# Grid attention of a four-block transformer kernel: values stationary in column halves, probabilities normalised first, attention gates projected turned

## The chip, the cores and the metric

One core of one Trainium2 chip runs the whole program in one launch. The time is the device time of one execution in microseconds (us); lower is better. Three runs of the kernel before took 1077.77, 1074.63 and 1081.78 us, median 1077.77.

## The reference

The reference applies a first block of two layers (retention, sparse attention and a gated linear attention, merged by gates) to 256 tokens of width 1024, and then a second block of two layers to these 256 tokens and 256 context tokens. The change lies in the second block's first layer, `even_layer`. Cut to what matters, for 512 rows (four tiles of 128: tiles 0 and 1 are the sequence, 2 and 3 the context):

```python
q, k, v, u, vv, gate = split(h @ w_in)         # widths 512, 128, 128, 512, 512, 1024
# 8 heads of 64, 2 key/value heads; a learned sink logit for each head
s = [q @ k.T * scale (masked to a window for the sequence), sink]
p = softmax(s)[..., :-1]                       # the sink takes its share, and is dropped
a = p @ v                                      # 512 wide
b = gelu(u) * spatial_mix(layer_norm(gelu(vv)))# 512 wide
y = (concat([a, b]) * silu(gate)) @ w_out      # 1024 -> 1024
x = x + gate_ada * y
```

A sequence tile attends to all four tiles under a mask, a context tile to the two context tiles.

## The kernel before, in words

Five instruction streams are written out by hand: SyncE issues the weight transfers into a ring of three 2 MB slots, TensorE multiplies, VectorE and ScalarE evacuate the eight PSUM banks, GpSimd does a little. Every PSUM use is a named unit in a fixed list (`units_of_layer_e` for this layer): the list sets which bank a unit has and, bank by bank, the order. `filled(engine, unit)` waits until TensorE has written a unit, `emptied` until its reader has freed the bank. Each engine's stream is in the order in which it is written; nothing overtakes.

Projections that must be exact to float32 are made of three products of a faster type: `hi*hi`, `hi*rest`, `low*hi`. For that ScalarE copies each operand into a rounded high half (`wide_high`, L1709) and VectorE subtracts it from the original to get the low half (`wide_low`, L2508). A weight chunk comes in four pieces, and `project_wide` (L1113) waits for piece k/2 before its products 3k. Its stationary operand is the tokens' 128x128 block, its moving one 512 weight columns: 24 products a tile.

The grid attention runs in 15 steps, the loops over `E_STEPS` in the streams of TensorE (L1240), ScalarE (L1769) and VectorE (L2589). There are 24 units: one head of a sequence tile over 512 keys (0 to 15), or two heads of a context tile over 256 keys each (16 to 23). Step g handles:

- the gate projection of `E_GATES`: attention half (`e_g0`) in steps 0 to 3, the other half (`e_g1`) in steps 7 to 10, one tile a step; ScalarE takes its tanh, VectorE makes silu of it in `eg` (`e_silu`);
- modulation rows (`ada_rows`, `ada`, `mod_out`) in steps 5 to 11 and two row products (`gate_rows`) in each of steps 11 and 12, in banks 0 and 1 by turns with the gates;
- the transposes of units 2g-4 and 2g-3 (`e_turn`), copied out by ScalarE into `PT2e`;
- the logits of units 2g and 2g+1 (`e_logits_pair`), which VectorE evacuates with the mask (L2602) and reduces to the maximum (L2605), or reduces straight from PSUM (L2609); ScalarE then takes the exponential in place with the row sum (L1789, L1794);
- the values of units 2g-6 and 2g-5 (`e_values`): stationary is the transposed block of probabilities, 128x128, moving are 64 columns of `ev`;
- in step 4 the spatial gate's products (L1275), four units of two products in banks 0 and 1, multiplied out of PSUM by VectorE (L2631);
- the split of the next gate or output weights: ScalarE in steps 4, 5, 10, 11; VectorE in steps 5, 6 (`e_g1`), 11 and 12 (first output half).

The probabilities are not normalised before the values: `e_gated` (L2546) adds the sink's exponential to the row sums, takes the reciprocal, multiplies a tile's 512 attended columns out of PSUM by it, and then by the gate. The tile's 1024 mixed columns are turned with eight transposes in two banks (`turn_mixed`), split into high (`mixed_high`) and low (`mixed_low`) halves, and projected (`project_mixed`): tile 0 in step 14, the rest behind the loop. The float32 products of attention appear as two instructions each in the trace, the transposes as one. The second attention, in the layer after (`o_values` L1372, `o_normal` L2721), already has normalised probabilities moving over stationary values.

Of the kernel before, what the change touches and what calls it, by code (L numbers as in the profile page):

```python
# [215 lines left out]
def units_of_layer_e():  # L216
# [17 lines left out]
    for g in range(E_STEPS):  # L234
# [63 lines left out]
def build(nc, x, weights, cols, k1, gmask, ident_in, wlr, context, k2, out):  # L298
    ctx = ExitStack()
    with ctx:  # L300
# [142 lines left out]
        eg = sbe("eg", [P, NT, D])  # L443
# [25 lines left out]
        etmp = evv[:, 0, :]  # L469
# [69 lines left out]
        def e_rows(name):  # L539
            return eg[:, int(name[-1]), 0:512] if name in E_EARLY.values() else msum2[E_ROWS.index(name) % 2]  # L540
# [163 lines left out]
        def _(pe):  # L704
# [420 lines left out]

            def project2(u, name, slot, t, width):
# [59 lines left out]
            def e_turn(i):  # L1186
                if E_UNITS[i][0] < TT:
                    pe.wait_ge(event("e_exp"), i + 1)
                else:
                    emptied(pe, u, f"el{i}")  # L1190
                ps = begin(u, f"ep{i}")
                done(u, f"ep{i}", turn_blocks(ps, [L2e[:, i % 4, b * P:(b + 1) * P] for b in range(4)]))

            def e_values(i):
                emptied(pe, u, f"ep{i}")
                t, heads = E_UNITS[i]
                b0 = 0 if t < TT else TT
                nb = NT - b0
                if i == 0 or E_UNITS[i - 1][0] != t:
# [6 lines left out]
                if i == E_LAST[t]:  # L1206
# [18 lines left out]
            def turn_mixed(t):  # L1225

                pe.wait_ge(event("em_ready"), t + 1)
                pe.wait_ge(event("eb_ready"), t + 1)
                for h in range(2):
                    ps = begin(u, f"eyT{t}{h}")  # L1230
                    done(u, f"eyT{t}{h}", turn_blocks(ps, [eg[:, t, (4 * h + i) * P:(4 * h + i + 1) * P] for i in range(4)]))

            def project_mixed(h, t):

                if h == 0:
                    emptied(pe, u, f"eyT{t}0")
                    emptied(pe, u, f"eyT{t}1")
                project_wide(u, f"eout{t}{h}", 2 + h, t)

            for g in range(E_STEPS):  # L1240
                if g in E_GATES:
                    n, t = E_GATES[g] // 4, E_GATES[g] % 4
                    project_wide(u, f"e_g{n}{t}", n, t)
# [18 lines left out]
                if g >= 3:  # L1262
                    e_values(2 * g - 6)
                    e_values(2 * g - 5)
# [133 lines left out]
        def _(act):  # L1398
# [322 lines left out]
            def mixed_high(t):  # L1721

                for h in range(2):
                    ps = filled(act, u, f"eyT{t}{h}")
                    act.activation(xhi[:, 4 * h:4 * h + 4, t * P:(t + 1) * P], ps[:, :].rearrange("p (k c) -> p k c", k=4),
                                   ACT.Copy).then_inc(event("yhi_ready"), 1)
# [42 lines left out]
            for g in range(E_STEPS):  # L1769
                if g in E_GATES:  # L1770
                    n, t = E_GATES[g] // 4, E_GATES[g] % 4
                    ps = filled(act, u, f"e_g{n}{t}")
                    act.activation(eg[:, t, n * 512:(n + 1) * 512], ps[:, :], ACT.Tanh, scale=0.5).then_inc(event("e_tanh"), 1)
# [9 lines left out]
                if g < 12:  # L1783
                    for i in (2 * g, 2 * g + 1):
# [6 lines left out]
                        else:  # L1791
# [6 lines left out]
                            ins.then_inc(free(u, f"el{i}"), 1)  # L1798
                for j, n in {4: ((1, 0), (1, 1)), 5: ((1, 2), (1, 3)), 10: ((2, 0), (2, 1)), 11: ((2, 2), (2, 3))}.get(g, ()):
# [3 lines left out]
                for t in range(NT):  # L1803
                    if g == E_LAST[t] // 2 + 1:
                        act.wait_ge(event("e_arg"), t + 1)
                        act.activation(es2[:, t, :], es2[:, t, :], ACT.Exp).then_inc(event("e_es"), 1)
# [216 lines left out]
        def _(dve):  # L2023
# [521 lines left out]

            def e_gated(t):  # L2546

                dve.wait_ge(event("e_es"), t + 1)
                if t < TT:
# [340 lines left out]
```

## Time and profile before

| | |
|---|---|
| profiled execution | 1075.43 us |
| its span in the trace | 1073.5 us |
| granted TensorE clock, mean | 0.996 |
| TensorE busy | 1037.6 us, 97% |
| VectorE busy | 600.8 us, 56% |
| ScalarE busy | 477.8 us, 45% |
| GpSimd busy | 76.4 us, 7% |

The page gives each engine's busy time, the span in forty slices, the chain of waits that ended last, and the costliest groups of instructions by line and shape. PE is TensorE's matmul stream, PEld its weight loads (which overlap it), DVE is VectorE, ACT is ScalarE. A matmul's recorded length holds its latency, so instructions in a row overlap in the record: their price is the distance from one start to the next. The same holds, to 0.08 us, on VectorE.

### The profile page before, as it was taken

The page shows a single profiled execution, that of the slowest core. Times are in us where ns is not written, and L with a number is a line of the kernel's source. Part 1 is how long each engine was busy: PE and PEld are TensorE (multiplying, and loading weights), DVE is VectorE, ACT ScalarE, POOL GpSimd, SP SyncE. Part 2 cuts the span into 40 slices and gives each one's busy share as a digit, 9 for nine tenths or more (in the row PEclk, how much of TensorE's full clock was granted, in tenths as well). Part 3 has the DMA queues.
Part 4 walks back from the last instruction along what each step waited for, and adds up shares of the span by engine and source line. Part 5 has one row for each costly group of instructions (what it writes and reads, how often), then busy time and mean ns, then how long its engine had stood idle before and what let it go on. Part 6 is the DMA issues. An engine that isn't in the chain of part 4 may idle for free.

```text
span 1073.5 us, 13401 instructions
## 1 busy us (share of the span) xinstructions
PE 1037.6 (97%) x5148; PEld 751.6 (70%) x5148; DVE 600.8 (56%) x1177; ACT 477.8 (45%) x942; POOL 76.4 (7%) x103
## 2 busy tenths in 40 slices
PE   7999999999999999999999999999999999999997
PEld 5788875777466887757774587777677888556553
DVE  2539866595756299764455744235745555245742
ACT  3436546562144375375630353245535423225641
POOL 3001110000000021100000000500000001230000
PEclk9999999999999999999999999999999999999999
DMA  9844442477615454326467352431642016242000
GB/s 387 315 197 158 157 158 79 157 313 296 250 55 196 178 198 173 124 112 233 170 251 288 135 222 79 157 108 70 235 157 104 1 40 228 106 157 99 1 1 39
DMA packets 13742, 171.27 MB, mean 160 GB/s; under 512 B 1504, under 2 KB 1760, under 8 KB 3056
## 3 DMA queue, kind: packets, MB, share of 16 engines
q1 hardware_dynamic: 13216, 168.82, 41.2%
q10 hardware_dynamic: 464, 1.61, 0.4%
q8 instruction: 41, 0.67, 0.3%
q14 instruction: 21, 0.17, 0.0%
HBM read 169.37 MB, written 1.05 MB: 159 GB/s over the span
## 4 chain that ended last, share of the span: by engine, by line
PE 83%; DVE 7%; ACT 7%; DMA 2%; issue 1%; SPq 0%; DVEq 0%; ACTq 0%
PE bank L785 15%; PE bank L1123 8%; PE bank L1072 8%; PE bank L1012 7%; PE bank L1170 6%; PE bank L756 5%; PE bank L1129 5%; PE bank L1105 4%; PE bank L763 3%; PE bank L1307 3%; PE bank L857 3%; PE bank L1384 2%; PE bank L719 2%; PE bank L1372 1%; PE bank L727 1%
## 5 line engine op out<-in xcount | busy, mean ns | idle before, releaser
L1496 ACT ACTIVATE whi<-ring 128x512 fp32r<-128x512 f32 x120 | 73.8, 629 | 67.7 <-PE bank L785 67.5
L785 PE MATMUL bank<-whi,xhi 128*128 128x512 f32 (+1 forms) x256 | 99.2, 388 | 1.3 <-ACT dsag L1419 1.3
L2160 DVE TENSOR_TENSOR wlo<-ring,whi 128x512 fp32r<-128x512 f32 x120 | 82.2, 707 | 29.7 <-ACT whi L1496 29.4
L785 PE MATMUL bank<-whi,xlo 128*128 128x512 f32 (+1 forms) x256 | 97.9, 382 | 0.0
L785 PE MATMUL bank<-wlo,xhi 128*128 128x512 f32 (+1 forms) x256 | 97.4, 381 | 0.0
L763 PE MATMUL bank<-ring,hT 128*128 128x512 f32 (+1 forms) x160 | 61.8, 540 | 1.8 <-ACT hT L1439 1.8
L1129 PE MATMUL bank<-ring,hT 128*128 128x256 f32 (+2 forms) x224 | 57.9, 418 | 3.3 <-ACT hT L1462 2.3
L1012 PE MATMUL bank<-merge_high,xhi 128*128 128x512 f32 x144 | 58.5, 406 | 1.6 <-ACT retqkv L1419 1.1
L1012 PE MATMUL bank<-merge_high,xlo 128*128 128x512 f32 x144 | 57.0, 396 | 0.0
L785 PEld LDWEIGHTS bank<-whi,xhi 128*128 128x128 f32 x256 | 48.1, 188 | 12.7 <-ACT dsag L1419 1.6
L1012 PE MATMUL bank<-ring_low,xhi 128*128 128x512 f32 x144 | 56.7, 394 | 0.0
L785 PEld LDWEIGHTS bank<-wlo,xhi 128*128 128x128 f32 x256 | 48.2, 188 | 9.9
L785 PEld LDWEIGHTS bank<-whi,xlo 128*128 128x128 f32 x256 | 48.1, 188 | 9.9
L1129 PEld LDWEIGHTS bank<-ring,hT 128*128 128x128 f32 x224 | 38.9, 190 | 21.4 <-issue 16.3
L2349 DVE TENSOR_TENSOR ring_low<-ring,merge_high 128x1024 fp32r<-128x1024 f32 x36 | 42.5, 1222 | 18.8 <-ACT merge_high L1596 18.6
L1123 PE MATMUL bank<-ring_low,xhi 128*128 128x512 f32 x128 | 50.4, 394 | 0.0
L763 PEld LDWEIGHTS bank<-ring,hT 128*128 128x128 f32 x160 | 29.7, 190 | 28.6 <-issue 20.1
L1654 ACT ACTIVATE out_high<-ring 128x1024 fp32r<-128x1024 f32 x16 | 15.6, 1045 | 65.4 <-DMA ring<-in_weights 65.4
L2061 DVE SCALAR_TENSOR_TENSOR retqkv<-ring,cst,retqkv 128x512 f32<-128x512 f32 x56 | 42.1, 752 | 2.0
L1596 ACT ACTIVATE merge_high<-ring 128x1024 fp32r<-128x1024 f32 x36 | 36.0, 1052 | 9.7 <-PE bank L1012 9.7
L1123 PE MATMUL bank<-wide,xhi 128*128 128x512 f32 x96 | 39.0, 406 | 0.2 <-DVE ring_low L2511 0.2
L1170 PE MATMUL bank<-whi,xhi 128*128 128x512 f32 x96 | 38.4, 400 | 0.0
(412 smaller groups left out, 2182.4 us busy)
## 6 DMA issues: line engine op xcount, KB each, us to landing
ring<-in_weights SPq DMA_DIRECT2D x73, 2048.0 KB, 8.1
ring<-in_weights SPq DMA_DIRECT2D x5, 1024.0 KB, 5.1
ring<-in_weights SPq DMA_DIRECT2D x2, 1360.0 KB, 10.0
ring<-in_weights SPq DMA_DIRECT2D x1, 1536.0 KB, 8.7
kk<-in_k SPq DMA_DIRECT2D x1, 1120.0 KB, 8.1
X<-in_x SPq DMA_DIRECT2D x1, 1024.0 KB, 14.7
kc<-in_k ACTq DMA_DIRECT2D x1, 1024.0 KB, 11.9
X<-in_context SPq DMA_DIRECT2D x1, 1024.0 KB, 10.0
```

The lines of the kernel that those rows point to most:

```text
L756: mm = pe.transpose(ps[0:n, i * P:(i + 1) * P], blk, ident[:])
L763: mm = pe.matmul(ps[:, 0:width], hT[:, k, t * P:(t + 1) * P], ring[:, slot, k * width:(k + 1) * width], start=(k == 0), stop=(k == KD - 1))
L785: mm = pe.matmul(o[:, 0:width], a, b[:, q % BUFFERS, at], start=(k == 0 and m == 0), stop=(k == KD - 1 and m == 2))
L1012: mm = pe.matmul(o[:, :], a, b, start=(k == 0 and n == 0), stop=(k == KD - 1 and n == 2))
L1072: mm = pe.matmul(ps[:, :], branchT[b][:, k, t * P:(t + 1) * P], ring[:, slot, k * D + h * 512:k * D + h * 512 + 512], start=(k == 0), stop ...
L1105: mm = pe.matmul(ps[:, :], a, b, start=(k == 0 and m == 0), stop=(k == KD - 1 and m == 2))
L1123: mm = pe.matmul(ps[:, :], a, b, start=(k == 0 and n == 0), stop=(k == KD - 1 and n == 2))
L1129: mm = pe.matmul(ps[:, 0:width], hT2[:, k, t * P:(t + 1) * P], ring[:, slot, k * width:(k + 1) * width], start=(k == 0), stop=(k == KD - 1))
L1170: mm = pe.matmul(o[:, :], a, b, start=(k == 0 and m == 0), stop=(k == KD - 1 and m == 2))
L1496: act.activation(whi1[:, q % BUFFERS, :], w, ACT.Copy).then_inc(event("hi1_ready"), 1)
L2160: dve.tensor_tensor(wlo1[:, q % BUFFERS, :], piece1(q)[2], whi1[:, q % BUFFERS, :], ALU.subtract).then_inc(event("lo1_ready"), 1)
L2349: dve.tensor_tensor(rest, w, whole, ALU.subtract).then_inc(event("merge_low"), 1)
```

## The change

The values become the stationary operand, 128x64, in the left or right half of the array's columns by the parity of the head, and the transposed probabilities move over them, 128 columns at a time; two units (an even and an odd head) alternate product by product. The result is the attended block turned: head dimension on partitions, tokens in columns. For that the probabilities are normalised before they are turned (`e_normal`, VectorE, once a step for the step before), and the sink's argument and exponential are computed once a step for two or four heads (L2615 and L1806 before, once a tile). The gates' attention half is projected turned as well (`gates_e`: weights stationary, all 512 tokens moving). The gate is then multiplied in one instruction, and the high and low halves for the output projection are made from SBUF (`attended_high`, `attended_low`); only the other 512 columns are transposed, into one bank instead of two.

Where the pieces stand: `gates_e` in steps 0 to 3 on TensorE; the wait for `ea_low` in `project_mixed`, for h = 0; ScalarE's exponential of the sink behind each step's exponentials, `attended_high` in steps 9, 11, 14 and behind the loop; on VectorE `e_normal(g - 1)` at the head of steps 1 to 12, the sink's argument in every step behind the maxima, `e_gated` in steps 8, 10, 13 and behind the loop as before, `attended_low` in steps 10, 12, 14 and behind the loop.

```diff
     def units_of_layer_e():
         if g in E_TURNED:
-            u += [(f"eyT{E_TURNED[g]}{h}", (4, 0)[E_TURNED[g]] + h) for h in range(2)]
-    u += [(f"eyT{t}{h}", (4, 0)[t % 2] + h) for t in range(2, NT) for h in range(2)]
+            u.append((f"eyT{E_TURNED[g]}", (5, 1)[E_TURNED[g]]))
+    u += [(f"eyT{t}", (5, 1)[t % 2]) for t in range(2, NT)]
...
-        eg = sbe("eg", [P, NT, D])
+        egT = sbe("egT", [P, 4, NT * P])
+        eb = sbe("eb", [P, NT, 512])
...
+            def gates_e(j):
+                ps = begin(le, f"e_g0{j}")
+                for k in range(KD):
+                    if k % 2 == 0:
+                        pe.wait_ge(event("wide_low"), k // 2 + 1)
+                    at = k * 512 + j * P
+                    whole, rest = wide[:, k, j * P:(j + 1) * P], ring_low[:, SLOT2["e_g0"], at:at + P]
+                    for n, (a, b) in enumerate(((whole, xhi), (rest, xhi), (whole, xlo))):
+                        mm = pe.matmul(ps[:, :], a, b[:, k, :], start=(k == 0 and n == 0), stop=(k == KD - 1 and n == 2))
+                done(le, f"e_g0{j}", mm)
...
             def e_turn(i):
-                if E_UNITS[i][0] < TT:
-                    pe.wait_ge(event("e_exp"), i + 1)
-                else:
-                    emptied(pe, u, f"el{i}")
+                pe.wait_ge(event("e_norm"), i + 1)
...
-            def e_values(i):
+            def e_values(g):
+                units = (2 * g, 2 * g + 1)
...
-                for a, h in enumerate(heads):
+                for a in range(len(E_UNITS[units[0]][1])):
                     for b in range(nb):
-                        mm = pe.matmul(o[:, h * 64:(h + 1) * 64], PT2e[:, i % 4, (a * nb + b) * P:(a * nb + b + 1) * P],
-                                       ev[:, b0 + b, (h // 4) * 64:(h // 4) * 64 + 64], start=(b == 0), stop=(b == nb - 1))
+                        for r, i in enumerate(units):
+                            h = E_UNITS[i][1][a]
+                            mm = pe.matmul(o[64 * r:64 * r + 64, (h // 2) * P:(h // 2 + 1) * P],
+                                           ev[:, b0 + b, (h // 4) * 64:(h // 4) * 64 + 64],
+                                           PT2e[:, i % 4, (a * nb + b) * P:(a * nb + b + 1) * P],
+                                           start=(b == 0), stop=(b == nb - 1))
...
             def turn_mixed(t):
-                pe.wait_ge(event("em_ready"), t + 1)
                 pe.wait_ge(event("eb_ready"), t + 1)
-                for h in range(2):
-                    ps = begin(u, f"eyT{t}{h}")
-                    done(u, f"eyT{t}{h}", turn_blocks(ps, [eg[:, t, (4 * h + i) * P:(4 * h + i + 1) * P] for i in range(4)]))
+                ps = begin(u, f"eyT{t}")
+                done(u, f"eyT{t}", turn_blocks(ps, [eb[:, t, i * P:(i + 1) * P] for i in range(4)]))
...
+                    pe.wait_ge(event("ea_low"), t + 1)
...
+            def attended_high(t):
+                emptied(act, u, f"eo{t}")
+                c = slice(t * P, (t + 1) * P)
+                act.activation(xhi[:, 0:4, c], egT[:, :, c], ACT.Copy).then_inc(event("ea_high"), 1)
...
+                    act.wait_ge(event("e_arg"), g + 1)
+                    t, heads = step_heads(g)
+                    act.activation(es2[:, t, heads], es2[:, t, heads], ACT.Exp).then_inc(event("e_es"), 1)
...
+            def e_normal(g):
+                t, heads = step_heads(g)
+                dve.wait_ge(event("e_es"), g + 1)
+                if t < TT:
+                    dve.wait_ge(event("e_exp"), 2 * g + 2)
+                else:
+                    emptied(dve, u, f"el{2 * g}")
+                    emptied(dve, u, f"el{2 * g + 1}")
+                step(dve.tensor_tensor(r2[:, t, heads], sm2[:, t, heads], es2[:, t, heads], ALU.add))
+                settle()
+                step(dve.reciprocal(r2[:, t, heads], r2[:, t, heads]))
+                settle()
+                for i in (2 * g, 2 * g + 1):
+                    n = 512 // len(E_UNITS[i][1])
+                    for a, h in enumerate(E_UNITS[i][1]):
+                        v = L2e[:, i % 4, a * n:(a + 1) * n]
+                        ins = dve.tensor_scalar(v, v, r2[:, t, h:h + 1], None, ALU.mult)
...
             def e_gated(t):
-                step(dve.tensor_tensor(r2[:, t, 0:8], sm2[:, t, 0:8], es2[:, t, :], ALU.add))
-                step(dve.reciprocal(r2[:, t, 0:8], r2[:, t, 0:8]))
-                dve.tensor_tensor(etmp.rearrange("p (h d) -> p h d", h=8), ps[:, :].rearrange("p (h d) -> p h d", h=8),
-                                  r2[:, t, 0:8].unsqueeze(2).broadcast_to([P, 8, 64]), ALU.mult).then_inc(free(u, f"eo{t}"), 1)
-                dve.scalar_tensor_tensor(eg[:, t, 0:512], etmp, 0.5, eg[:, t, 0:512], ALU.mult, ALU.mult).then_inc(event("em_ready"), 1)
+                v = egT[:, :, t * P:(t + 1) * P]
+                dve.scalar_tensor_tensor(v, ps[:, :].rearrange("p (j c) -> p j c", j=4), 0.5, v, ALU.mult,
+                                         ALU.mult).then_inc(free(u, f"eo{t}"), 1)
+
+            def attended_low(t):
+                dve.wait_ge(event("ea_high"), t + 1)
+                c = slice(t * P, (t + 1) * P)
+                dve.tensor_tensor(xlo[:, 0:4, c], egT[:, :, c], xhi[:, 0:4, c], ALU.subtract).then_inc(event("ea_low"), 1)
...
-                for t in range(NT):
-                    if g == E_LAST[t] // 2:
-                        dve.wait_ge(event("e_max"), E_LAST[t] + 1)
-                        dve.tensor_tensor(es2[:, t, :], mx2[:, t, 0:8], sink, ALU.add).then_inc(event("e_arg"), 1)
+                    dve.wait_ge(event("e_max"), 2 * g + 2)
+                    t, heads = step_heads(g)
+                    dve.tensor_tensor(es2[:, t, heads], mx2[:, t, heads], sink[:, heads], ALU.add).then_inc(event("e_arg"), 1)
```

## Rows read from the trace of the kernel before

**Rows 1.** The page: busy us, share of the span, instructions of each engine.

```profile
PE 1037.6 (97%) x5148; PEld 751.6 (70%) x5148; DVE 600.8 (56%) x1177; ACT 477.8 (45%) x942; POOL 76.4 (7%) x103
```

**Rows 2.** Busy time by stretch (columns in its first line), steps 4 and 5.

```profile
core 0: us, PE busy (x) PEld busy (x) DVE busy (x) ACT busy (x) POOL busy (x), PEclk, DMA share, GB/s
755.00:771.00 16.00, 14.76 (x102) 10.44 (x100) 11.86 (x26) 8.18 (x17) 0.00 (x0) 1.00 0.56 222
```

**Rows 3.** The chain of waits, 754 to 784: start us, us, what.

```profile
754.23 0.70 DVE hT L2602
...
757.39 0.17 DVE es L2615
...
758.95 0.61 DVE hT L2602
...
761.99 0.80 DVE eu L2631 x2
...
769.05 0.70 DVE hT L2602
...
777.55 1.15 DVE ring_low L2511
```

**Rows 4.** Timeline of TensorE, 757 to 776: start us, us, what [idle before].

```profile
758.00 2.00 PE L1204 MATMUL bank<-ev,hT 128*128 128x64 f32 x16
759.84 1.95 PE L1275 MATMUL bank<-evv,ring 128*128 128x256 f32 x8
762.83 1.99 PE L1275 MATMUL bank<-evv,ring 128*128 128x256 f32 x8 [1.04 <-DVE eu L2631]
...
775.52 0.48 PE L1123 MATMUL bank<-wide,xhi 128*128 128x512 f32 x1
```

**Rows 5.** Weight loads of two lines (ns min/median/max), and timeline of tiled products.

```profile
L1204 PEld LDWEIGHTS bank<-ev,hT x192: 186/192/193, 754.1 to 845.1; 128*128 128x128 f32 x192
...
L1372 PEld LDWEIGHTS bank<-LP,ova x128: 132/137/137, 989.8 to 1036.6; 128*64 128x64 f32 x128
...
489.44 0.71 PE L940 MATMUL bank<-Y,KL 64*128 64x128 f32 x8
490.09 0.50 PE L1012 MATMUL bank<-merge_high,xhi 128*128 128x512 f32 x1
...
996.98 1.95 PE L1372 MATMUL bank<-LP,ova 128*64 128x256 f32 x16
998.86 1.09 PE L756 MATMUL bank<-ident,LP 128*128 128x128 f32 x8
```

**Rows 6.** Timeline of ScalarE: the end of step 3's exponentials.

```profile
758.02 0.19 ACT L1789 ACTIVATION_READ_ACCUMULATOR hT<-hT,mx 128x1 f32 x1
```

**Rows 7.** Timeline of VectorE: steps 3 and 11, and the second attention.

```profile
752.94 0.69 DVE L2570 SCALAR_TENSOR_TENSOR eg<-eg,bank 128x512 f32<-128x512 f32 x1 [1.87 <-ACT eg L1773]
...
829.27 4.62 DVE L2511 TENSOR_TENSOR ring_low<-ring,wide 128x1024 fp32r<-128x1024 f32 x4
...
983.22 0.89 DVE L2729 TENSOR_SCALAR LP<-LP,r 128x512 f32<-128x512 f32 x2
984.01 1.28 DVE L2736 TENSOR_REDUCE mx<-bank 128x1 f32<-128x512 f32 x2
```

**Rows 8.** The chain of waits, 815 to 845.

```profile
822.27 0.17 DVE r L2553
...
822.70 0.70 DVE evv L2558
...
824.15 0.18 DVE mod L2048
...
838.11 5.57 PE bank L1123 x24
```

**Rows 9.** Timeline of TensorE, steps 12 and 13.

```profile
831.85 1.90 PE L1204 MATMUL bank<-ev,hT 128*128 128x64 f32 x16
833.58 1.04 PE L756 MATMUL bank<-ident,eg 128*128 128x128 f32 x8
834.46 1.04 PE L756 MATMUL bank<-ident,hT 128*128 128x128 f32 x8
```

More of the change, by code:

```diff
@@ L539, in e_rows, with step_heads @@
         def e_rows(name):
-            return eg[:, int(name[-1]), 0:512] if name in E_EARLY.values() else msum2[E_ROWS.index(name) % 2]
+            return egT[:, int(name[-1]), :] if name in E_EARLY.values() else msum2[E_ROWS.index(name) % 2]
+        def step_heads(g):
+            t, heads = E_UNITS[2 * g]
+            return t, slice(heads[0], E_UNITS[2 * g + 1][1][-1] + 1)
         def e_which(name):
@@ L1242, in _ @@
                     n, t = E_GATES[g] // 4, E_GATES[g] % 4
-                    project_wide(u, f"e_g{n}{t}", n, t)
+                    if n == 0:
+                        gates_e(t)
+                    else:
+                        project_wide(u, f"e_g1{t}", 1, t)
                 if g in E_SUMS:
@@ L1262, in _ @@
                 if g >= 3:
-                    e_values(2 * g - 6)
-                    e_values(2 * g - 5)
+                    e_values(g - 3)
                 if g in E_TURNED:
@@ L1721, in mixed_high @@
             def mixed_high(t):
[L1723 to L1726, printed above, removed]
+                ps = filled(act, u, f"eyT{t}")
+                act.activation(xhi[:, 4:KD, t * P:(t + 1) * P], ps[:, :].rearrange("p (k c) -> p k c", k=4),
+                               ACT.Copy).then_inc(event("yhi_ready"), 1)
+            def attended_high(t):
+                emptied(act, u, f"eo{t}")
+                c = slice(t * P, (t + 1) * P)
+                act.activation(xhi[:, 0:4, c], egT[:, :, c], ACT.Copy).then_inc(event("ea_high"), 1)
             def e_sums_out(name):
@@ L1772, in _ @@
                     ps = filled(act, u, f"e_g{n}{t}")
-                    act.activation(eg[:, t, n * 512:(n + 1) * 512], ps[:, :], ACT.Tanh, scale=0.5).then_inc(event("e_tanh"), 1)
+                    act.activation((eb if n else egT)[:, t, :], ps[:, :], ACT.Tanh, scale=0.5).then_inc(event("e_tanh"), 1)
                 if g in E_SUMS:
@@ L2544, in spatial_norm @@
                 dve.tensor_tensor(evv[:, t, :], evv[:, t, :], lnb, ALU.add).then_inc(event("ln_ready"), 1)
[L2546 to L2563 removed]
+            def e_normal(g):
[3 more added lines that the diff above has]
+                    dve.wait_ge(event("e_exp"), 2 * g + 2)
+                else:
+                    emptied(dve, u, f"el{2 * g}")
[9 more added lines that the diff above has]
+                        ins = dve.tensor_scalar(v, v, r2[:, t, h:h + 1], None, ALU.mult)
+                        if a < len(E_UNITS[i][1]) - 1:
+                            step(ins)
+                    ins.then_inc(event("e_norm"), 1)
@@ L2568, in e_silu @@
                 ps = filled(dve, u, f"e_g{n}{t}")
-                v = eg[:, t, n * 512:(n + 1) * 512]
+                v = (eb if n else egT)[:, t, :]
                 dve.scalar_tensor_tensor(v, v, 1.0, ps[:, :], ALU.add, ALU.mult).then_inc(free(u, f"e_g{n}{t}"), 1)
@@ L2576, in e_mixed @@
                 emptied(dve, u, f"e_g1{t}")
-                v = eg[:, t, 512:1024]
+                v = eb[:, t, :]
                 dve.scalar_tensor_tensor(v, eu[:, t, :], 0.5, v, ALU.mult, ALU.mult).then_inc(event("eb_ready"), 1)
             def mixed_low(t):
-                for h in range(2):
-                    dve.wait_ge(event("yhi_ready"), 2 * t + h + 1)
-                    ps = filled(dve, u, f"eyT{t}{h}")
-                    c = slice(t * P, (t + 1) * P)
-                    dve.tensor_tensor(xlo[:, 4 * h:4 * h + 4, c], ps[:, :].rearrange("p (k c) -> p k c", k=4),
-                                      xhi[:, 4 * h:4 * h + 4, c], ALU.subtract).then_inc(free(u, f"eyT{t}{h}"), 1)
+                dve.wait_ge(event("yhi_ready"), t + 1)
+                ps = filled(dve, u, f"eyT{t}")
+                c = slice(t * P, (t + 1) * P)
+                dve.tensor_tensor(xlo[:, 4:KD, c], ps[:, :].rearrange("p (k c) -> p k c", k=4),
+                                  xhi[:, 4:KD, c], ALU.subtract).then_inc(free(u, f"eyT{t}"), 1)
             for g in range(E_STEPS):
+                if 1 <= g < 13:
+                    e_normal(g - 1)
                 if g in E_GATES:
@@ L2639, in _ @@
                     e_gated({8: 0, 10: 1, 13: 2}[g])
+                if g in (10, 12, 14):
+                    attended_low({10: 0, 12: 1, 14: 2}[g])
                 if g in E_TURNED:
@@ L2657, in _ @@
                             mixed_low(t + 2)
+                            if t == 0:
+                                attended_low(3)
                         elif t == 2:
```

30 lines of the change are left out of this document (11 added, 19 removed).

## The prediction, before the result was known

> **What bounds the kernel now.** I read the page's busy times first: TensorE is busy for 97% of the span [rows 1], so any work taken from it looks like time won. The change lies in the grid attention, about 725 to 888 us. The second view, busy time by stretch, already warns [rows 2]: at 755 to 771 TensorE is idle for 1.24 us of 16 while VectorE works 11.86, and the granted clock is 1.00, so no idle time is to be blamed on the clock. The third view settles it. The chain of waits [rows 3] runs through VectorE, not TensorE, from 754.23 to 762.78 (evacuations, maxima, two layer-norm instructions, the next step's evacuations, the first spatial-gate product), then through VectorE again from 769.05 to 778.70. Its last pieces there are the low half of a gate weight, for which TensorE's gate waits. TensorE is 97% busy and yet, in steps 4 to 6, VectorE sets its pace: from 754.23 to 763 it has next to no gap. The question is therefore what the change adds to VectorE ahead of those two points, and not only what it takes from TensorE.
>
> **What is removed from TensorE.** *Values.* There are 96 products, each two instructions, so 16 instructions in each of 12 steps. Now one step costs 1.84 us (758.00 to 759.84) [rows 4], in the last three steps 1.73 (831.85 to 833.58) [rows 9]. That is 0.115 us for 64 moving columns, while a full-width product with 256 columns costs 0.22 (eight in 1.99 with the last one's tail, from 762.83) [rows 4]. So it isn't the columns that cost here, but the 128-column weight load: 192 ns in length, against 137 for 64 columns [rows 5]. Afterwards the same 16 instructions have 64-column weights, 128 moving columns, and alternate between the two column halves of the array. The nearest row is the second attention's value product, with the same form and 256 columns: 16 in 1.88 us (996.98 to 998.86) [rows 5], 0.235 for a pair, about the price of one full-width instruction with 256 columns. The halves thus run side by side. With half the columns a pair costs about 0.11, and eight pairs 0.86; I take 1.0 us with the 0.12 to 0.16 us that the row has over eight times its streaming. From the other side, the row-halved product with 128 moving columns and 128-column loads took 0.65 us for eight (489.44 to 490.09) [rows 5], 1.3 us for 16; and no gain at all is 1.84. I take 1.0, since a 64-column load is the shorter one. Saved: 9 x 0.84 + 3 x 0.73 = 9.8 us.
>
> The pair row also speaks against a rule: 16 loads of the two halves lie beside streaming, as a pair costs no more than streaming its 256 columns. The Trainium skill (TensorE: Matmul & The Clock Gate, What overlaps and what doesn't) has a weight load overlap a running product only where its row group differs, and column halves share their row groups; the trace disagrees. By that rule load and streaming of a pair would add, about the 1.3 us a step of the row-halved product, and the change would give the third rival's time.
>
> *Transposes.* The mixed rows are now turned with 8 transposes a tile, 0.88 us (833.58 to 834.46) [rows 9]. Half of them go: 4 x 0.44 = 1.8 us.
>
> *Gates.* The attention half is projected turned: again 4 x 24 products, 128-column weights, 512 moving columns, and the same waits for weight pieces. Cost 0.
>
> TensorE loses 9.8 + 1.8 = 11.5 us of work (rounded once).
>
> **What is added to VectorE.** *Normalising*, once a step, at the head of the next step's queue: an addition and a reciprocal, 0.43 together (822.27 to 822.70) [rows 8], and the scaling of two 128x512 blocks in place. The second attention does just that scaling: two in 0.79 us (983.22 to 984.01) [rows 7]. So 1.22 us in steps 1 to 8. In the last four groups it is four blocks of 128x256, a form with no row: between half of 0.395 and all of it; I take 0.25 each, 1.4 us in all (bounds 1.2 and 2.0). *The sink's argument*, now in every step: 0.2 (0.17 at 757.39, and 0.02 of issue ahead of it) [rows 3], new in 8 of 12. *Gating* falls from four instructions, 1.88 us (822.27 to 824.15) [rows 8], to one of 0.65 (its 0.69 in the rows of that form less the overlap with the next). The low halves for the output projection stay 8 in number, four of them now from SBUF: no change. ScalarE gets 8 more small exponentials (under 0.2 each) and keeps its 8 high halves; it is busy for 8.18 of the 16 us of the tightest stretch [rows 2], so 0. SP and the weight transfers aren't touched; slots come free with TensorE's projections and move with them.
>
> New waits: VectorE now waits for ScalarE's exponentials before evacuating the next logits. In step 3 these end at 758.21 [rows 6], VectorE reaches the wait at 758.95 [rows 3]: no stall. In step 4 and after it gets there later still.
>
> **The walk**, each shift against the time before:
> - Steps 0 to 3: VectorE has a gap of 1.87 us ahead of its gate product [rows 7] and takes the 1.4 in. 0.
> - Step 4: it is back to back from 754.23. Group 3's scaling and one argument come ahead of the first spatial-gate evacuation: +1.42. TensorE, 1.68 us early from two cheaper value steps, waits longer instead: it goes on at 764.25, not 762.83, and into step 5 at +1.42.
> - Steps 5 and 6: TensorE would reach step 7's gate at 775.52 + 1.42 - 1.68 = 775.3 and want the third weight piece 12 products later, 2.8 us by the gate's 5.57 for 24 [rows 8], at 778.1. That piece was ready at 778.70. Ahead of it VectorE now has +1.42, two arguments and group 5's scaling: 0.4 + 1.22, in all +3.04, ready at 781.8. The gate ends 3.04 late. The four value steps have won nothing.
> - Steps 7 to 9: VectorE waits for gates here, so 3 x 0.84 is real: +0.52 at step 10's logits.
> - Step 11: the second row product waits for VectorE to empty a bank (824.15 and 0.18) [rows 8]. Before that now: -1.88 + 1.26 (gating and a low half) + 0.2 (argument) + 1.4 (group 10's scaling) = +0.98. Shift +1.50.
> - Step 13: the last group's turn needs its scaling, which stands behind step 11's three weight pieces. The pieces start at 829.27 and take 3.46 of the 4.62 for four [rows 7]: 832.73 + 1.50, and 0.43 + 0.5 for the first unit make 835.2. TensorE would be there at 834.46 + 1.50 - 0.84 - 0.73 - 0.44 = 833.95 [rows 9]. It waits 1.2: shift +0.74.
> - Step 14: one value step and one tile's transposes less, but the projection (838.11 before) needs VectorE's last piece and two low halves, ready at 835.66 + 1.15 + 2 x 0.61 = 838.0: shift 0.0.
> - After that 0.73 of values and 2 x 0.44 of transposes, all real, with 5.57 us of projection to cover every low half: **-1.6 us**. What follows is bound as before and only moves.
>
> Of 11.5 us, 9.9 go into waits for VectorE. The profiled execution took 1075.4 (span 1073.5); 1073.8 after. The median of the runs, 1077.8, lies 2.3 above it; so 1076.2, and I say **1076 us**.
>
> **Rivals.**
> 1. *The work taken from TensorE is won whole*, -11.5, 1066.3 us. For it: TensorE's 97%. Against it: the two stretches in which the chain runs on VectorE [rows 3]. It takes VectorE having 3 us more slack than those rows show. 0.07.
> 2. *Slower: the two column halves don't overlap at 128 columns*, each step's values still cost 1.84, and VectorE's additions stay. By the same walk: +3.04 after step 7, +4.02 after step 11, then only transposes are won, 4 x 0.44: +2.3, 1080.1 us. It decides from 1.44 us a value step upwards, where the sum is zero. With 128x256 scalings at 0.4 it becomes +3.4. Against it: the pair row. 0.17.
> 3. *The halves overlap in part*, 1.3 us a step: by the walk +1.4 at step 10, +0.8 at step 14, -0.6 at the end, 1077.2 us. 0.14.
>
> The forecast has the remaining 0.62.
>
> **How the numbers follow.** Forecast and rivals 2 and 3 lie between -1.6 and +3.4. The runs before spread over 7.2 us, so a median can lie 3 off its place, and a stall of the walk may be missed by 3 either way: 1069 to 1083 holds all but rival 1 and a little on each side. A measurement of this kernel can tell about 1%, 10.8 us, from no change. Only rival 1 passes that: faster 0.07. Slower by 10.8 would take a stall in every step that no row shows: 0.03. Same 0.90.
>
> **What would show it.** In the profile after: value steps of 16 instructions in about 1.0 us (else rivals 2, 3); TensorE idle before the second half of the spatial-gate products for about 3.5 us instead of 1.04, and inside step 7's gate for about 3.5 instead of 0.2, both released by VectorE (else rival 1); about 2.3 us idle before the second row product of step 11; a wait of TensorE for the last group's scaling. TensorE's busy time should fall by roughly 10 us with the span nearly unmoved. The forecast is wrong if ScalarE's exponentials hold VectorE back in the short steps, or if the scaling in place costs more than 0.4 us a block.

## The result, and the profile after

| | before | after |
|---|---|---|
| median of 20 executions each, same chip | 1077.35 us | 1079.91 us |
| lowest to highest | 1074.63 to 1081.78 | 1076.62 to 1084.95 |
| profiled execution (span) | 1075.43 (1073.5) | 1078.6 (1076.6) |
| its mean granted clock | 0.996 | 0.992 |

The ratio is 1.0029, 95% interval 1.0017 to 1.0042: 3.1 us slower by the ratio (2.6 by the medians), where 1.6 us faster was forecast. The time lies inside the stated range, but the sign is wrong. Three executions of the batches below took much longer than the rest of their kernel's (2127 us in before_pad6, 1771 in the kernel before, 1090 in no_scaling) and are left out of every comparison. The busy times of the page (as [rows 1]):

```profile
PE 1032.2 (96%) x5132; PEld 739.9 (69%) x5132; DVE 612.3 (57%) x1229; ACT 478.5 (44%) x950; POOL 76.5 (7%) x103
```

TensorE is busy for 5.4 us less, VectorE for 11.5 us more, ScalarE for 0.7 more. The forecast wanted TensorE lower by about 10; that some 5 of them are missing is a first hint that part of its work ran longer. From the grid attention's first logits to the end of its output projection the kernel before needs 156.95 us (730.86 to 887.81), the one after 158.90 (732.22 to 891.12): +1.95. It also enters that stretch 1.36 us later than before, ahead of the changed code. Ahead of it the granted clock fell once in the profile of before (0.62 at 236 to 240 us) and twice in that of after (0.64 at 8 to 12, 0.60 at 336 to 340), so not every fall of the clock comes from the change; the sums below leave this offset out.

The timeline of TensorE after the change (columns as in [rows 4]), steps 3 to 5 and 7:

```profile
758.98 1.10 PE L1223 MATMUL bank<-hT,ev 128*64 128x128 f32 x16
760.38 1.97 PE L1296 MATMUL bank<-evv,ring 128*128 128x256 f32 x8 [0.30 <-issue]
765.53 2.48 PE L1296 MATMUL bank<-evv,ring 128*128 128x256 f32 x8 [3.19 <-DVE eu L2677]
767.94 3.08 PE L724 MATMUL bank<-ring,cst 128*32 128x512 f32 x16
770.94 1.09 PE L761 MATMUL bank<-ident,hT 128*128 128x128 f32 x8
...
777.02 1.09 PE L1223 MATMUL bank<-hT,ev 128*64 128x128 f32 x16
778.05 0.50 PE L1128 MATMUL bank<-wide,xhi 128*128 128x512 f32 x1
...
780.70 0.40 PE L1128 MATMUL bank<-wide,xlo 128*128 128x512 f32 x1
784.39 0.80 PE L1128 MATMUL bank<-wide,xhi 128*128 128x512 f32 x1 [3.30 <-DVE ring_low L2539]
784.98 0.63 PE L1128 MATMUL bank<-ring_low,xhi 128*128 128x512 f32 x1
...
788.73 1.92 PE L724 MATMUL bank<-ring,cst 128*32 128x512 f32 x16
```

A value step takes 1.03 us (777.02 to 778.05), as forecast. The two waits for VectorE are there, in the places and nearly the sizes of the walk: 3.19 + 0.30 against "about 3.5", 3.30 against "about 3.5". Now look at what stands *behind* each. The same 16 modulation rows take 3.00 us after the first wait (767.94 to 770.94) and 1.85 after the second gate (788.73 to 790.58). The first gate products after the second wait go 0.43 apart, the later ones 0.23. The same places in the kernel before:

```profile
765.02 1.92 PE L719 MATMUL bank<-ring,cst 128*32 128x512 f32 x16 [0.20 <-DVE eu L2631]
766.87 1.09 PE L756 MATMUL bank<-ident,hT 128*128 128x128 f32 x8
...
778.74 0.50 PE L1123 MATMUL bank<-wide,xhi 128*128 128x512 f32 x1 [0.20 <-DVE ring_low L2511]
...
781.72 1.92 PE L719 MATMUL bank<-ring,cst 128*32 128x512 f32 x16
```

The busy time by stretch has the reason in the column PEclk:

```profile
core 0: us, PE busy (x), PEclk, DMA share, GB/s
762.00:766.00 4.00, 0.81 (x4) 1.00 0.00 0
766.00:770.00 4.00, 4.00 (x20) 0.61 0.27 57
780.00:784.00 4.00, 1.09 (x5) 1.00 0.02 8
784.00:788.00 4.00, 3.61 (x10) 0.58 0.00 0
```

The granted clock was 1.00 (2.4 GHz) in the slices that hold the waits and 0.61 and 0.58 in those behind them, where TensorE was back at work: for most of these it stood at the lower level, 1.2 GHz. Against the kernel before, from start to start: spatial products 2.41 (765.53 to 767.94) instead of 2.19, modulation rows 3.00 instead of 1.85, the gate's second half 4.34 (784.39 to 788.73) instead of 2.98. That is **2.7 us** that no instruction count shows.

The waits of TensorE, 755 to 845 (us in total, times, longest):

```profile
PE bank L1128 <- DVE ring_low L2539: 3.3, 1, 3.3
PE bank L1296 <- DVE eu L2677: 3.2, 1, 3.2
PE bank L1159 <- DVE mod L2076: 2.5, 1, 2.5
PE bank L761 <- ACT hT L1440: 1.6, 1, 1.6
```

The third is step 11's (forecast 2.3), and here the clock stayed at 1.00. The fourth is step 13's, and its releaser is not the one forecast. The chain of waits there, answering to [rows 8]:

```profile
834.51 1.56 ACT hT L1820 x7
836.07 0.09 ACT es L1827
836.16 1.89 ACT wide L1740 x2
838.05 0.52 ACT xhi L1752
838.57 0.97 ACT gbr L1440 x2
839.54 0.50 ACT hT L1440
840.04 0.14 issue
840.18 1.11 PE bank L761 x8
```

TensorE waits for ScalarE's copy of the turned probabilities, and ScalarE was busy without a break: exponentials, two high halves of weights, a high half of attended values, two copies of row products, all ahead of it in its queue. VectorE's scaling of the last group began only at 838.82, so it was late too, but not last. Step 14's projection starts at 842.90. By the walk (no shift), the later entry of 1.36 and the clock's 2.7 it should have been at 842.2: **0.7 us**, put down to that queue.

So the profiled stretch adds up: -1.6 by the walk, +2.7 clock, +0.7 ScalarE's queue, in all +1.8 against +1.95 measured.

### The profile page after: what moved, and what is told of

The parts are those of the page before. It is cut to its first block, busy times and chain, and to the rows that moved or that the text cites. A ratio compares the mean times of both kernels' runs of the same rounds, so it can differ in the third digit from the quotient of the medians.

```text
span 1076.6 us, 13435 instructions
## 1 busy us (share of the span) xinstructions
PE 1032.2 (96%) x5132; PEld 739.9 (69%) x5132; DVE 612.3 (57%) x1229; ACT 478.5 (44%) x950; POOL 76.5 (7%) x103
## 4 chain that ended last, share of the span: by engine, by line
PE 78%; DVE 9%; ACT 7%; DMA 4%; issue 2%; SPq 0%; DVEq 0%; ACTq 0%
PE bank L790 15%; PE bank L1077 6%; PE bank L1187 6%; PE bank L1128 6%; PE bank L1017 5%; PE bank L761 5%; PE bank L1146 5%; PE bank L1110 4%; PE bank L768 3%; PE bank L1328 3%; PE bank L862 3%; DMA ring<-in_weights 2%; PE bank L1405 2%; PE bank L1140 2%; DVE retqkv L2089 2%; PE bank L724 2%
## 5 line engine op out<-in xcount | busy, mean ns | idle before, releaser
L1017 PE MATMUL bank<-ring_low,xhi 128*128 128x512 f32 x144 | 56.0, 389 | 0.0
L1128 PE MATMUL bank<-ring_low,xhi 128*128 128x512 f32 x96 | 38.4, 400 | 0.0
L2534 DVE TENSOR_TENSOR ring_low<-ring,whi 128x1024 fp32r<-128x1024 f32 x12 | 15.6, 1297 | 39.3 <-ACT whi L1728 39.3
```

The lines of the kernel that those rows point to most:

```text
L1017: mm = pe.matmul(o[:, :], a, b, start=(k == 0 and n == 0), stop=(k == KD - 1 and n == 2))
L1128: mm = pe.matmul(ps[:, :], a, b, start=(k == 0 and n == 0), stop=(k == KD - 1 and n == 2))
```

## The experiments

Two theories stood against each other. *The clock:* the walk is right, and the new waits of TensorE cost their length and then a second time, in a lower clock behind them. *Missed work:* the change adds something that the walk has too cheap (the scalings, or halves that overlap less than thought). Each ratio is taken against the kernel before in the same batch, on the same chip. "Below after" sets medians of different batches beside each other; the kernel before lay between 1076.8 and 1077.4 us in them.

Beside its time each execution lists its mean granted clock. (1 - clock) x span is the full-speed time withheld from it. It is the most that the clock can cost: over the grid attention 3.4 us were withheld in the profile of after, and 2.7 show in the durations. One value is coarse (0.001 is 1.1 us), a mean over many executions is less so: before 6.1 us (5.6 to 6.8 in three later batches; the first lists no clocks for it), after **9.8**. The difference of the means without that time is -0.3 us (1071.2 and 1070.9), and the walk with ScalarE's 0.7 gives -0.9; the kernel before itself lies between 1070.7 and 1071.6 in this figure. In these means the clock accounts for up to 3.7 us, more than the whole loss.

**pieces_first.** In step 6 VectorE makes the two low halves that step 7's gate wants ahead of the scaling and the evacuations.

```diff
             for g in range(E_STEPS):
+                if g == 6:
+                    wide_low(1, 2)
+                    wide_low(1, 3)
                 if 1 <= g < 13:
                     e_normal(g - 1)
...
-                for j, n in {5: ((1, 0), (1, 1)), 6: ((1, 2), (1, 3)), 11: ...
+                for j, n in {5: ((1, 0), (1, 1)), 11: ...
```

> Theory A (the changed kernel loses because VectorE's new work delays it at two places, and TensorE, having waited over 3 us there, then runs at 1.2 GHz for some us): with VectorE's last two gate-weight pieces (1,2) and (1,3) ahead of step 6's scaling and evacuations, TensorE's 3.30 us wait inside step 7's gate goes to under 0.5, the granted clock stays 1.00 behind it and the gate's second half takes 2.8 us again instead of 4.40. The wait before the spatial gate's second half (3.2) and its fall of the clock stay. Against the changed kernel: -3.3 and -1.6, about -5 us; against the kernel before about -2 us. Theory B (the loss is added latency spread over all steps, such as ScalarE's and VectorE's waits on each other; or the time before this layer): the wait goes, but shows up again at the next place, and the time moves by less than 1.5 us.

Measured: 1075.70 us, ratio 0.9987 (0.9968 to 1.0006), 4 us below after, where about 5 were expected. The gate's wait is gone, and with it the slow products behind it. But the mean withheld is still 9.3 us: what was won is the wait, and none of the clock's part can be seen in the means. The spatial wait stayed at 3.19 us, and this is the surprise of its timeline:

```profile
764.50 1.99 PE L1296 MATMUL bank<-evv,ring 128*128 128x256 f32 x8 [3.19 <-DVE eu L2680]
766.70 1.92 PE L724 MATMUL bank<-ring,cst 128*32 128x512 f32 x16 [0.20 <-DVE eu L2680]
...
822.81 1.12 PE L1159 MATMUL bank<-Y,ones 128*128 128x512 f32 x2 [2.46 <-DVE mod L2076]
823.77 1.49 PE L761 MATMUL bank<-ident,hT 128*128 128x128 f32 x8
825.20 2.08 PE L1241 MATMUL bank<-ekT,eqT 64*128 64x256 f32 x8
```

Behind the same wait, the same rows took 1.92 and not 3.08. In this execution the clock fell behind step 11's wait instead (transposes 1.43 for 0.97, logits 2.00 for 1.06), where the profile of after had none. Which wait is followed by a fall differs from one execution to the next.

**spatial_first.** Group 3's scaling goes behind the spatial-gate products in step 4.

```diff
-                if 1 <= g < 13:
+                if 1 <= g < 13 and g != 4:
                     e_normal(g - 1)
...
                         ins.then_inc(free(u, f"gs{j}"), 1)
+                    e_normal(3)
```

> Theory A: with group 3's normalising behind the spatial gate's multiplications in step 4, the wait before the second half of the spatial-gate products falls from 3.2 to about 2.0 us. If a wait of about 2 us leaves the clock alone (as the 2.46 us wait of step 11 did), the four products take 0.9 us and the modulation rows behind them 1.86 instead of 3.01: -1.2 and -1.7, about -3 us against the changed kernel, less what then turns up at step 7's gate, where the wait stays above 3. If the clock still falls: -1.2. Theory B: no change.

Measured: 1076.95 us, ratio 1.0005 (0.9987 to 1.0022), 3 us below after. The wait fell from 3.19 to 2.00, as a scaling of 1.22 predicts, and the clock did not fall behind it in the profile:

```profile
769.32 1.99 PE L1296 MATMUL bank<-evv,ring 128*128 128x256 f32 x8 [2.00 <-DVE eu L2677]
```

The gate's 3.3 us is untouched, and its profile has the clock down behind that wait and again at 832 to 838, behind step 11's. The mean withheld is 7.3 us.

**before_pad3, before_pad6.** The clock alone, without the change: in the kernel *before*, three or six idle scalings on VectorE ahead of its multiplications of the spatial-gate products in step 4. TensorE's work is unchanged.

```diff
                 if g == 4:
+                    for j in range(3):      # 6 in before_pad6
+                        settle()
+                        step(dve.tensor_scalar(gbr[:, j % 2, 0:512], lng, 1.0, None, ALU.mult))
                     for j in range(4):
```

> The kernel before with three idle scalings of a 128x512 block (1.2 us of VectorE, into an unused buffer) ahead of the spatial gate's multiplications of step 4: this makes the wait alone, without the rest of the change. The wait before the second half of the products grows from 1.04 to 2.3 us, and by the chain through VectorE the time grows by 1.2 us. If the wait is followed by TensorE at 1.2 GHz in part of the executions, the median grows by more than that, up to 3.

> The same with six scalings, 2.4 us: the wait grows to about 3.5 us, longer than the changed kernel's 3.19. A wait that costs only its own length makes the time 2.5 us longer. If TensorE's clock falls behind such a wait, as in the profile of the changed kernel, the spatial products and the modulation rows take up to 1.4 us more in the executions where it does: 2.5 to 4 us.

Measured: pad3 1080.81 us, ratio 1.0037 (1.0021 to 1.0053), +4.0 us by the ratio and 3.7 by the medians, above the 3 expected at most. Its wait grew by 1.25, from 1.04 to 2.29, and behind it:

```profile
765.45 2.59 PE L1275 MATMUL bank<-evv,ring 128*128 128x256 f32 x8 [2.29 <-DVE eu L2634]
767.98 2.96 PE L719 MATMUL bank<-ring,cst 128*32 128x512 f32 x16
```

Over this stretch its granted clock is 0.59:

```profile
core 0: us, PE busy (x), PEclk, DMA share, GB/s
766.00:770.00 4.00, 4.00 (x19) 0.59 0.32 66
```

The mean full-speed time withheld is 8.5 us, 2.9 more than in the kernel before of the same batch (5.6). 1.25 of waiting cost 4.0 in time: here the clock's share is shown without the change. pad6 gave 1080.65 us, ratio 1.0032 (1.0021 to 1.0043), +3.4 for twice the padding, with 7.4 withheld. A longer wait is not seen to cost more clock, but 7.4 and 8.5, from nine executions each, are not told apart by their spread either. pad6 has no row to show: its one profile is of the execution of 2127 us, in which TensorE was busy 99% of the time, and nothing here explains that.

**before_pieces_first.** The control: the same reordering as pieces_first, in the kernel before.

> The kernel before with the two gate-weight pieces at the head of step 6 on VectorE, as in the reordered version of the changed kernel. In the kernel before TensorE waits 0.20 us there, so the order alone can give 0.2 us: no change that can be measured. If it gained 3 us or more, the reordered kernel's 6.4 us would be the order's and not the change's.

Measured: 1076.40 us, ratio 0.9996 (0.9984 to 1.0008). TensorE's waits there stay 1.0, 0.7 and 0.2. This order by itself is worth nothing that can be measured; it pays only where the change has made the wait.

**no_scaling.** The change without the multiplications of the probabilities, so that its attended values stay unnormalised; the sums, the reciprocals and all waits are kept.

```diff
-                step(dve.reciprocal(r2[:, t, heads], r2[:, t, heads]))
-                settle()
-                for i in (2 * g, 2 * g + 1):
...
-                    ins.then_inc(event("e_norm"), 1)
+                dve.reciprocal(r2[:, t, heads], r2[:, t, heads]).then_inc(event("e_norm"), 2)
```

> The changed kernel without the 32 scalings of the probabilities (the values stay unnormalised; sink sum and reciprocal are kept, and so are all the waits). The scalings are 0.79 us of VectorE a step. If VectorE's work ahead of the two waits is what costs, both waits shrink by 0.8 us (3.2 to 2.4 and 3.3 to about 2.5), and by the walk the time falls 2.7 us; with waits this much shorter the clock falls less often, up to 2.7 us more. So -2.7 to -5.5 against the changed kernel, 0 to -3 against the kernel before. If the loss sat in the waits between ScalarE and VectorE and not in the scaling's length, the time stays within 1 us of the changed kernel's.

Measured: 1077.21 us, ratio 1.0000 (0.9985 to 1.0016), 2.7 us below after, as the walk has it. Waits of 2.4 and 2.3 us are left, and 10.0 us are still withheld by the clock. Without the clock's part its mean is 4.0 us below the kernel before of the same batch, where the walk (1.6 and 2.7, less ScalarE's 0.7) has 3.6. The scalings cost what the walk had for them, and with all of them gone the kernel is still no faster than the one before, though TensorE has 11.5 us less work: against *missed work* in the scalings, and for the clock.

**halves_apart.** The two column halves are no longer alternated: eight instructions of one, then eight of the other (for a context tile, four by four).

```diff
-                    for b in range(nb):
-                        for r, i in enumerate(units):
+                    for r, i in enumerate(units):
+                        for b in range(nb):
```

> The four products of one column half in a row, then the four of the other, where the changed kernel alternates. If alternating is what lets the halves run side by side, a value step costs 1.7 to 1.9 us instead of 1.03, as in the kernel before; by the walk +4.0 us against the changed kernel with the clock as it is. But TensorE then comes later to the two waits (about 2.4 and 1.9 us); if these are short enough for the clock to stay at 2.4 GHz, 3.3 us come back and the time is about +1. If the time per step is still 1.03, the saving was the 64-column load's and not the side-by-side running, and the time is as the changed kernel's.

Measured: 1081.53 us, ratio 1.0040 (1.0023 to 1.0057), 1.6 us above after. The value step:

```profile
757.37 1.58 PE L1223 MATMUL bank<-hT,ev 128*64 128x128 f32 x16
758.88 1.09 PE L761 MATMUL bank<-ident,hT 128*128 128x128 f32 x8
```

1.51 us instead of 1.03; 1.7 to 1.9 were expected. Of the 0.81 us that a step won against 1.84 [rows 4], 0.48 comes from alternating the halves and 0.33 from the rest of the new form (64-column weights, 128 moving columns). And of 12 x 0.48 = 5.8 us of TensorE work added, only 1.6 appear in the time: VectorE sets the pace. The walk, whose sum is zero at 1.44 us a step, would put this kernel about 2 us above after. The waits shrank to 3.0, 2.3 and 2.0 us, but the clock did not come back: 10.0 us are withheld, and the profile has it down behind the first and the third.

**copies_first.** ScalarE's part only: in step 12 the copies of the turned probabilities go ahead of the second modulation rows, one attended tile's high half goes a step later, and its low half on VectorE behind that of the turned rows.

```diff
-                if g in E_ROWS_AT:
-                    v = E_ROWS_AT[g]
+                if g == 11:
                     for h in range(2):
-                        copy_out(u, f"gb{v}{h}", ...
+                        copy_out(u, f"gb0{h}", ...
                 if 2 <= g < 14:
                     ...
+                if g == 12:
+                    for h in range(2):
+                        copy_out(u, f"gb1{h}", ...
...
-                    attended_high({9: 0, 11: 1, 14: 2}[g])
+                    attended_high({9: 0, 12: 1, 14: 2}[g])
```

> Only ScalarE's order in step 12: the copies of the transposes come ahead of the row products' copies, and the second tile's high half behind them (its low half on VectorE follows the first tile's). In the profile of the changed kernel TensorE waits 1.57 us in step 13, and the releaser is ScalarE's copy. If that queue is what holds it, the wait falls to the 0.9 us or so that group 11's scaling still needs and the time falls 0.8 us; the prediction's own account (the scaling alone is late) has no change. Either lies near the limit of what 5 rounds can tell, so the wait in the profile decides.

Measured: 1078.24 us, ratio 1.0012 (0.9998 to 1.0026), 1.7 below after, with 9.2 withheld. The other three waits are unchanged (3.3, 3.2, 2.5), and step 13's now ends by the scaling:

```profile
PE bank L761 <- DVE hT L2593: 0.9, 1, 0.9
```

**two_places** joins spatial_first and pieces_first; **reordered** adds to them copies_first and, in steps 6, 8, 9 and 11, the emptying of the modulation bank ahead of the scaling. reordered_again is the same program in a second batch.

```diff
+                if 1 <= g < 13 and g != 4 and g not in E_ADA:
                     e_normal(g - 1)
...
                 if g in E_ADA:
                     mod_out(u, E_ADA[g], int(E_ADA[g][-1]), e_which(E_ADA[g]), (1, 2))
+                    e_normal(g - 1)
```

> Theory A: both of these reorderings, the bank-freeing instruction of the modulation rows ahead of the scaling in steps 6, 8, 9 and 11, and in step 12 ScalarE copying the transposes before the row products, with the second tile's high half behind them. By the walk, with value steps of 1.03: -6.9 us of waits, and -3.3 if the clock stays up: about -10 against the changed kernel, -7 against the kernel before. Remaining waits: about 2 us in step 4, 0.9 in step 11, 0.9 in step 13. Theory B: within 2 us of the changed kernel.

> Both reorderings on VectorE in steps 4 and 6, and nothing else. By the walk -4.7 us against the changed kernel without the clock (the sum of its parts is -1.2 and -3.5), and back to the kernel before's clock cost where the two waits of over 3 us are gone: another -2 to -4. So 1071 to 1074 us. The wait of 2.46 us in step 11 stays, and with it some executions with the clock down there.

> The fully reordered kernel once more, for more executions beside the kernel before: 1070 to 1072 us, ratio 0.994 within 0.001. It should lie 1 to 2 us below the kernel with the two reorderings alone, which is what the rest (step 11's bank, step 12's copies) is worth by the walk: 2.2 us.

Measured: two_places 1074.83 us, ratio 0.9978 (0.9965 to 0.9991), just above the 1071 to 1074 expected; reordered 1070.39, 0.9938 (0.9917 to 0.9960), and again 1070.22, 0.9938 (0.9923 to 0.9952). That is 4.5 us below two_places, where 1 to 2 were expected. TensorE's waits in the last:

```profile
PE bank L1296 <- DVE eu L2683: 2.0, 1, 2.0
PE bank L1159 <- DVE mod L2078: 1.0, 1, 1.0
PE bank L761 <- DVE hT L2593: 0.9, 1, 0.9
```

Its stretch takes 149.36 us against 158.90, and no slice of it is below 1.00 in clock. The profile of the first batch has the same three waits, and there the clock did fall, behind the one of 1.00 us in step 11 (the transposes take 1.85 us from start to start instead of 0.97):

```profile
823.61 1.85 PE L1159 MATMUL bank<-Y,ones 128*128 128x512 f32 x2 [1.00 <-DVE mod L2078]
825.25 1.91 PE L761 MATMUL bank<-ident,hT 128*128 128x128 f32 x8
```

The mean withheld is 7.1 us in the first batch and 5.9 in the second, 6.5 together, near the kernel before's 6.1. two_places, whose step 11 still waits for 2.5 us (the clock fell there in its profile), has 9.8, as much as after: one wait gone and one shortened won 5 us, and none of it is clock. **reordered beats both kernels, by 6.7 us the one before**: with VectorE's new work placed behind what TensorE waits for, the change does save time. ScalarE's new order was not tried in the kernel before; its profile has no wait of TensorE in steps 12 and 13 that it could remove.

The time withheld, side by side; the last column is from one profile each, 724 to 896 us:

| kernel | mean of all executions, us | in the grid attention, us |
|---|---|---|
| before | 6.1 | 0 |
| before_pieces_first | 5.8 | 0 |
| before_pad3 | 8.5 | 1.7 |
| after | 9.8 | 3.4 |
| pieces_first | 9.3 | 1.7 |
| spatial_first | 7.3 | 5.1 |
| no_scaling | 10.0 | 1.7 |
| halves_apart | 10.0 | 3.4 |
| copies_first | 9.2 | 3.4 |
| two_places | 9.8 | 3.4 |
| reordered, two batches | 7.1, 5.9 | 1.7, 0 |

Each mean is uncertain by 0.3 us (before) to 1.3 (the last). Every profile with a wait of 2.3 us or more in this stretch has some clock lost in it; the two kernels whose longest wait is 1.04 us have none, and reordered, with 2.0, has it in one profile of two. How much each single wait costs cannot be read from these means.

## Why the prediction was wrong

*The step that failed* is the sum's treatment of waits. The prediction priced each new wait by its length, having set the clock aside ("the granted clock is 1.00, so no idle time is to be blamed on the clock"). That row [rows 2] was of a stretch whose longest wait was 1.04 us; the change put 3.19 and 3.30 us there and 2.46 in step 11. TensorE then ran at the lower level for some microseconds behind some of them: 2.7 us in the profiled execution, up to 3.7 in the mean of the executions. In the means the sum is -1.6, ScalarE's 0.7 and the clock's 3.7: +2.8 us, and the means of the first batch lie 2.7 apart (1077.9 and 1080.6). That a longer wait brings this cost is shown by before_pad3 (a longer wait and nothing else: +4.0, of which 1.25 is the wait); reordered agrees (the change's work all kept, the waits cut to 2.0 and less: 9.5 us below after, 3.3 of them clock, 9.8 less 6.5). Which of the three waits cost the clock is not shown: pieces_first and two_places, with one or two of them gone or cut, still have 9.3 and 9.8 withheld.

*A smaller step failed with it.* ScalarE's additions were set at 0 because it was busy for half of the tightest stretch. In step 13 it is busy all the time: it works back to back from 834.51 to 840.04, and the copy that the last turned group needs is last in line. 0.7 us in the profile; copies_first won 1.7 in the medians, more than this, and the excess lies within the spread (its ratio is known to 0.0014, 1.5 us).

*What was right.* The value step: 1.03 us for a forecast of 1.0. The scalings, from start to start: two 128x512 blocks in 0.80 us and the unseen form, four of 128x256, in 1.06 (the terms without their addition and reciprocal were 0.79 and 1.0). The shifts: less the 1.36 of the later entry TensorE goes on 1.34 us later at 765.53, where the walk has 1.42, and, less the 1.37 that the clock took on the way, 2.92 later at 784.39, where it has 3.04. The waits: 3.5, 3.5 and 2.3 forecast, 3.19 + 0.30, 3.30 and 2.46 measured. That nearly all of the 11.5 us would go into waits for VectorE was right too: with no clock cost the means lie 0.3 us apart.

*The rivals.* The first (all 11.5 won) is refuted by the waits of 3.19, 3.30 and 2.46 us, each ended by VectorE. The second forecast 1080.1, and the time came out at 1079.9, but for another reason: its value step of 1.84 us did not happen. A matching total doesn't confirm a mechanism. The third wanted 1.3 a step. The rule of the Trainium skill that it leaned on (TensorE: Matmul & The Clock Gate, The mechanism, under "What overlaps and what doesn't"), that a load overlaps a running product only across row groups, is not what the trace shows: alternating halves of the *columns*, with the same rows, brought the step from 1.51 to 1.03. The prediction's own estimate of the streaming alone, 0.86 for eight pairs, leaves 0.17 us of that for sixteen loads.

*Left open.* Why one and the same wait of 3.19 us is followed by a fall in one execution and by none in another; the profiles show that it is so, not what decides it. And the means of the kernel after without clock (-0.3) and of the walk with ScalarE's queue (-0.9) differ by 0.6, less than the 0.9 by which the batches of the kernel before differ in this figure.

## What to carry to other kernels

Where a change swaps TensorE work for waits of a microsecond or more, the sum isn't even: besides the length of the waits, allow for slower products behind them (here 1.4 us at each of the two places where the profile of after shows it, 2.9 us withheld in the mean for one padded wait, 3.7 for the whole change), and compare the executions' mean clocks. Before giving up such a change, look at what the releasing engine does just ahead of the release; moving the new work behind it, with ScalarE's copies moved ahead in one step, was worth 9.5 us here, with no instruction removed. And ask "is it busy" of an engine per step and per queue position, not per stretch.

## What the runs showed of the hardware

- Behind waits of 1.0 to 3.3 us TensorE's granted clock fell to 1.2 GHz for 3 to 7 us in some executions and not in others. It makes a good part of the spread: the lowest execution of after took 1076.6 us at a mean clock of 0.997, the highest 1085.0 at 0.989.
- In the profile of after the fall shows when TensorE is back at work, not in the wait: 1.00 at 762 to 766, 0.61 at 766 to 770.
- f32 products in the two column halves of the array, alternated, run side by side also at 128 moving columns: 16 in 1.03 us, 1.51 if not alternated.
- No more clock was lost with a longer padding than with a short one, within the spread (7.4 us withheld with six scalings, 8.5 with three).
